# Two of sixteen depthwise-convolution chunks as products with diagonal matrices on TensorE, in a two-layer encoder trunk

## The reference

```python
def conformer_conv(x, w_in, b_in, w_dw, b_dw, ln_g, ln_b, w_out, b_out):
    h = x @ w_in + b_in                       # (1, 256, 4096)
    a, gate = jnp.split(h, 2, axis=-1)
    h = a * jax.nn.sigmoid(gate)
    h = lax.conv_general_dilated(             # depthwise, causal, 31 taps
        h, w_dw, window_strides=(1,), padding=[(CONV_WIDTH - 1, 0)],
        feature_group_count=D_MODEL) + b_dw
    h = layer_norm(h, ln_g, ln_b)             # over the 2048 channels
    h = jax.nn.swish(h)
    return h @ w_out + b_out
```

## Time and profile before

| | |
|---|---|
| median of 3 runs | 3607.17 us (3604.32 to 3616.36) |
| the profiled execution | 3611.92 us, its span 3610.0 us |
| mean granted TensorE clock | 0.908 |
| busy | PE 2933.5 us, DVE 2580.9 us, Pool 1910.6 us, ACT 810.2 us |
| convolution module, up to the first layer norm | about the first 422 us of the span |

### The profile page before, as it was taken

One profiled execution on the slowest core, in us unless ns is written; L12 is line 12 of the kernel. 1 busy time (PEld: TensorE's weight loads), 2 busy tenths in 40 slices (PEclk: granted clock), 3 DMA queues, 4 the chain that ended last, 5 costly groups with the idle time before them and its releaser, 6 DMA issues.

```text
span 3610.0 us, 46542 instructions
## 1 busy us (share of the span) xinstructions
PE 2933.5 (81%) x15209; PEld 2256.1 (62%) x15209; DVE 2580.9 (71%) x3472; ACT 810.2 (22%) x1215; POOL 1910.6 (53%) x1526
## 2 busy tenths in 40 slices
PE   8977895767777789999399998957767777899994
PEld 7864695666767654444198886956666776544441
DVE  4997669787888776666744455697878887766667
ACT  1002431222333420000033443312223334300000
POOL 6795165777777554444300001547777775644443
PEclk9986997888989899999799999978889898999997
DMA  7421446999999669999855435459999997699998
GB/s 248 140 93 41 169 140 253 422 419 422 421 421 422 260 258 410 406 409 409 324 177 186 145 110 183 140 225 423 422 422 421 421 422 283 245 409 406 409 410 319
DMA packets 293734, 1106.84 MB, mean 307 GB/s; under 512 B 21957, under 2 KB 120837, under 8 KB 220677
## 3 DMA queue, kind: packets, MB, share of 16 engines
q0 software_dynamic: 147456, 805.37, 55.1%
q1 hardware_dynamic: 146182, 300.22, 23.1%
HBM read 1103.41 MB, written 2.10 MB: 306 GB/s over the span
## 4 chain that ended last, share of the span: by engine, by line
DMA 41%; PE 24%; DVE 20%; issue 9%; POOL 4%; ACT 1%; DVEq 0%; POOLq 0%; ACTq 0%; SPq 0%
DMA ring<-in_peer_u,index_now 21%; DMA work<-in_peer_v,index_add 14%; PE ps L631 8%; PE ps L651 7%; DMA more_add<-in_peer_v,index_add 6%; DVE work L1218 6%; DVE ps L1467 4%; PE ps L810 3%; POOL ring L544 3%; DVE ring L1424 2%; DVE x_tok L1309 1%; DVE hot_set L1487 1%; PE ps L695 1%; DVE work L1373 1%; DVE work L1370 1%
## 5 line engine op out<-in xcount | busy, mean ns | idle before, releaser
L1424 DVE SCALAR_TENSOR_TENSOR ring<-ring,x_tok 128x2048 f32<-128x2048 f32 x384 | 879.7, 2299 | 229.2 <-DMA ring<-in_peer_u,index_now 221.3
L544 POOL DMA_INDIRECT ring<-in_peer_u,index_now x512 | 843.2, 1647 | 367.1 <-issue 114.9
L849 PE MATMUL ps<-all_v,mix 128*128 128x512 f32 x1984 | 851.8, 592 | 0.0
L849 PEld LDWEIGHTS ps<-all_v,mix 128*128 128x128 f32 x1984 | 377.0, 190 | 474.5 <-issue 474.5
L816 PE MATMUL ps<-x_dot,work 128*128 128x128 f32 x4096 | 536.4, 294 | 94.3 <-ACT work L1066 65.6
L1467 DVE SCALAR_TENSOR_TENSOR ps<-work,coef,ps 128x1024 f32<-128x1024 f32 x344 | 442.2, 1289 | 233.1 <-DMA work<-in_peer_v,index_add 231.3
L810 PE MATMUL ps<-ident,ring 128*128 128x128 f32 x2048 | 348.4, 342 | 311.7 <-DMA ring<-in_peer_u,index_now 306.1
L816 PEld LDWEIGHTS ps<-x_dot,work 128*128 128x128 f32 x4096 | 518.9, 209 | 115.3 <-ACT work L1066 79.8
L810 PEld LDWEIGHTS ps<-ident,ring 128*128 128x128 f32 x2048 | 310.8, 179 | 333.8 <-DMA ring<-in_peer_u,index_now 194.7
L508 POOL TENSOR_TENSOR w_lo<-ring,w_hi 128x2048 fp32r<-128x2048 f32 x34 | 159.2, 4686 | 662.5 <-ACT w_hi L947 662.5
L590 POOL DMA_INDIRECT work<-in_peer_v,index_add x312 | 295.2, 946 | 316.9 <-DVE ps L1467 257.3
(11 more groups left out here) (183 smaller groups left out, 3682.3 us busy)
## 6 DMA issues: line engine op xcount, KB each, us to landing
all_v<-in_peer_v SPq DMA_DIRECT2D x248, 512.0 KB, 6.8
ring<-in_conv_w_in SPq DMA_DIRECT2D x16, 2048.0 KB, 8.8
ring<-in_peer_w_q SPq DMA_DIRECT2D x16, 2048.0 KB, 8.6
ring<-in_attn_w_kv SPq DMA_DIRECT2D x16, 2048.0 KB, 8.6
ring<-in_conv_w_out SPq DMA_DIRECT2D x8, 2048.0 KB, 7.9
ring<-in_attn_w_q SPq DMA_DIRECT2D x8, 2048.0 KB, 8.6
ring<-in_attn_w_o SPq DMA_DIRECT2D x8, 2048.0 KB, 7.9
ring<-in_peer_u,index_now POOLq DMA_INDIRECT x512, 15.0
```

The costliest lines, as they stand in the source:

```text
L544: pool.indirect_dma_start(u_tile(s), None, u_tab, bass.IndirectOffsetOnAxis(ap=index_now[:, half, s:s + 1], axis=0)).then_inc(u_row[s], 16)
L849: mm = pe.matmul(ps[:, dense_bank(tb, q), :], mix[tb][:, row, :], tile[:, q * 512 - HALF:(q + 1) * 512 - HALF], start=False, stop=True, sk ...
L1424: dve.scalar_tensor_tensor(out=u_tile(s), in0=u_tile(s), scalar=1.0, in1=x_tok[:, tb, :], op0=ALU.mult, op1=ALU.mult, accum_out=coef[:, tb ...
```

## The change

- Chunks 14 and 15 are convolved by PE: for each of 31 taps one product of a 128x128 diagonal matrix, which holds that tap of the 128 channels, with a shifted window of 256 columns of the gated, padded chunk, all accumulated in one PSUM bank (bank 4 or 5). ACT builds the diagonal matrices with 31 scaled copies of the identity for each chunk (`diagonals`): those of chunk 14 ahead of its sigmoids, those of chunk 15 after the last sigmoid. DVE takes each result from PSUM with one instruction that adds the bias and subtracts `pilot`.
- Chunk 12 goes from Pool to DVE. Pool has chunks 0, 4 and 8, DVE has eleven, PE two.
- The gates of the last group are moved: DVE gates 11, 12, 13 and 14 one behind the other ahead of the taps of chunk 11, and chunk 15 after them. Then follow chunk 12, the two results of PE, and chunk 13.
- PE convolves chunk 14 directly behind `hidden`, then chunk 15, then adds up twelve chunks (`EARLY_SUMS`), and only then writes the six residual banks; the sums of 12, 14, 15 and 13 follow.
- `load_rows(0)` moves on SP's queue from behind the first four panels to behind the second panel of `conv_w_out`, with a wait for PE's first chunk, because the matrices of chunk 14 lie in `ln_rows`. Those of chunk 15 lie in ring slot 2, so ACT's first rounding waits for PE's second chunk.

```diff
-CONV_ORDER = (0, 1, 2, 3, 4, 5, 6, 7, 9, 10, 11, 8, 13, 14, 12, 15)
+CONV_ORDER = (0, 1, 2, 3, 4, 5, 6, 7, 9, 10, 11, 8, 12, 14, 15, 13)
+SHIFT_ORDER = (9, 10, 11, 12, 14, 15, 13)
+PE_CHUNKS = (14, 15)
+EARLY_SUMS = 12
...
+        tap_diag = [nc.alloc_sbuf_tensor_at("tap_diag0", [P, W, P], F32, offset=ln_rows_at),
+                    nc.alloc_sbuf_tensor_at("tap_diag1", [P, W, P], F32, offset=ring_at + 4 * 2 * 2 * D)]
...
+        more_pad = view(18432, 3, PAD + S)
...
-            load_rows(0)
             sp.dma_start(bias_row[0:1, :], conv_b_out).then_inc(bias_loaded, 16)
...
                 load_split(conv_w_out[0], P_OUT + p, p, True)
+                if p == 1:
+                    sp.wait_ge(pe_conv, 1)
+                    load_rows(0)
...
-            convolve(2, 4)
+            convolve(2, 3)
...
             hidden(2, 4)
 
+            for n, k in enumerate(PE_CHUNKS):
+                pe.wait_ge(diag_ready, n + 1)
+                pe.wait_ge(glu_done, 4 + k + 1)
+                for w in range(W):
+                    mm = pe.matmul(ps[:, Q + n, 0:S], tap_diag[n][:, w, :], more_pad[:, 1 + n, w:w + S], start=(w == 0), stop=(w == W - 1))
+                mm.then_inc(pe_conv, 1)
...
-            pe.wait_ge(glu_done, 4 + KC)
-            pe.wait_ge(bias_loaded, 16)
-            for b in range(6):
-                residual_bias(b // Q, b % Q)
             pe.wait_ge(ch_steps, 1)
             for n, k in enumerate(CONV_ORDER):
+                if n == EARLY_SUMS:
+                    pe.wait_ge(glu_done, 4 + KC)
+                    pe.wait_ge(bias_loaded, 16)
+                    for b in range(6):
+                        if b >= Q:
+                            wait_shifted(pe, PE_CHUNKS[b - Q])
+                        residual_bias(b // Q, b % Q)
...
+            def diagonals(n):
+                for w in range(W):
+                    at = w * KC + PE_CHUNKS[n]
+                    last = act.activation(tap_diag[n][:, w, :], ident[:, :], ACT.Copy, scale=taps[:, at:at + 1])
+                last.then_inc(diag_ready, 1)
+            act.wait_ge(consts, 9)
+            diagonals(0)
...
+            act.wait_ge(proj, IN_HALVES)
+            diagonals(1)
...
                 if k == CONV_ORDER[-1]:
+                    act.wait_ge(pe_conv, 2)
                     for u in range(2):
                         round_half(U_OUT + u)
...
+            def convolve_last():
+                feed_pool(2)
+                for b in range(1, 4):
+                    at = (2 * 3 + b) * STEPS
+                    dve.wait_ge(conv_steps, at)
+                    gated(2, b, hpad[:, b % 2, PAD:])
+                    if b == 3:
+                        gated(3, 0, hpad[:, 0, PAD:])
+                        gated(3, 1, more_pad[:, 0, PAD:])
+                        gated(3, 2, more_pad[:, 1, PAD:])
+                    chunk_steps(2, b, at, hpad[:, b % 2, :], b % 2, True)
+                gated(3, 3, more_pad[:, 2, PAD:])
+                dve.wait_ge(conv_steps, 10 * STEPS)
+                chunk_steps(3, 0, 10 * STEPS, hpad[:, 0, :], 0, True)
+                for n, k in enumerate(PE_CHUNKS):
+                    dve.wait_ge(pe_conv, n + 1)
+                    dve.scalar_tensor_tensor(out=conv[:, k, :], in0=ps[:, Q + n, 0:S], scalar=vec[:, NB_IN + k:NB_IN + k + 1], in1=pilot,
+                                             op0=ALU.add, op1=ALU.subtract).then_inc(shifted, 1)
+                dve.wait_ge(conv_steps, 11 * STEPS)
+                chunk_steps(3, 1, 11 * STEPS, more_pad[:, 0, :], 1, True)
```

More of the change, by code:

```diff
@@ L236, in build @@
         conv_steps = sem("conv_steps")
+        diag_ready, pe_conv = sem("diag_ready"), sem("pe_conv")
         ch_stat, ch_steps, ch_act = sem("ch_stat"), sem("ch_steps"), sem("ch_act")
@@ L335, in wait_shifted @@
                 eng.wait_ge(shifted, k + 1)
-            elif k % 4 == 0:
-                eng.wait_ge(pool_free, 1 + k // 4 + 1)
+            elif k == KC // 2:
+                eng.wait_ge(pool_free, KC // 8 + 2)
             else:
-                eng.wait_ge(shifted, KC // 2 + (3 * (k // 4 - 2) + k % 4))
+                eng.wait_ge(shifted, KC // 2 + SHIFT_ORDER.index(k) + 1)
         block = ctx.enter_context(nc.Block())
@@ L1184, in _ @@
             dve.sem_inc(glu_done, 4)
+            dve.memset(more_pad[:, :, 0:PAD], 0.0)
             dve.memset(hpad[:, :, 0:PAD], 0.0).then_inc(conv_steps, W + 1)
@@ L1190, in _, with column, gated, feed_pool @@
             STEPS = W + 1
+            def column(at):
+                return vec[:, bass.ds(at, 1)] if not isinstance(at, int) else vec[:, at:at + 1]
+            def gated(i, b, to):
+                dve.wait_ge(sig_ready, i * 4 + (b + 1))
+                dve.scalar_tensor_tensor(out=to, in0=ps[:, b, 0:S], scalar=column(i * 4 + b),
+                                         in1=sig[:, b % 2, :], op0=ALU.add, op1=ALU.mult).then_inc(glu_done, 1)
+            def feed_pool(i):
+                dve.wait_ge(pool_free, i + 1)
+                gated(i, 0, pool_pad[:, PAD:])
+                dve.tensor_copy(pool_tap[:, 0:W], taps_by[:, :, bass.ds(i * 4, 1)].rearrange("p w c -> p (w c)")) \
+                   .then_inc(pool_fed, 1)
+                dve.tensor_copy(pool_tap[:, W:], column(i * 4 + NB_IN)).then_inc(pool_fed, 1)
@@ new lines, in chunk_steps @@
+            def chunk_steps(i, b, at, pad, e, shift):
+                dve.tensor_copy(tap_c[:, e, :], taps_by[:, :, bass.ds(i * 4 + b, 1)].rearrange("p w c -> p (w c)")) \
+                   .then_inc(conv_steps, 1)
+                dve.wait_ge(conv_steps, at + 1)
+                dve.wait_ge(glu_done, i * 4 + (4 + b + 1))
+                dve.tensor_scalar(acc_c[:, e, :], pad[:, 0:S], tap_c[:, e, 0:1],
+                                  column(i * 4 + (NB_IN + b)), ALU.mult, ALU.add).then_inc(conv_steps, 1)
+                chunk = conv[:, bass.ds(i * 4 + b, 1), :].rearrange("p a b -> p (a b)")
+                for w in range(1, W):
+                    dve.wait_ge(conv_steps, at + (1 + w))
+                    dve.scalar_tensor_tensor(out=acc_c[:, e, :] if w < W - 1 else chunk, in0=pad[:, w:w + S], scalar=tap_c[:, e, w:w + 1],
+                                             in1=acc_c[:, e, :], op0=ALU.mult, op1=ALU.add).then_inc(conv_steps, 1)
+                if shift:
+                    dve.wait_ge(conv_steps, at + STEPS)
+                    dve.tensor_tensor(out=chunk, in0=chunk, in1=pilot, op=ALU.subtract).then_inc(shifted, 1)
@@ L1191, in convolve @@
             def convolve(first, last):
                 with dve.Fori(first, last) as i:
[L1193 to L1200, removed]
@@ L1201, in convolve @@
-                    dve.tensor_copy(pool_tap[:, 0:W], taps_by[:, :, bass.ds(i * 4, 1)].rearrange("p w c -> p (w c)")) \
-                       .then_inc(pool_fed, 1)
-                    dve.tensor_copy(pool_tap[:, W:], vec[:, bass.ds(i * 4 + NB_IN, 1)]).then_inc(pool_fed, 1)
-                    for b in range(1, 4):
[L1205 to L1223, removed]
@@ new lines, in convolve @@
+                    feed_pool(i)
+                    for b in range(1, 4):
+                        at = i * (3 * STEPS) + b * STEPS
+                        dve.wait_ge(conv_steps, at)
+                        gated(i, b, hpad[:, b % 2, PAD:])
+                        chunk_steps(i, b, at, hpad[:, b % 2, :], b % 2, False)
+            def convolve_last():
+                feed_pool(2)
+                for b in range(1, 4):
+                    at = (2 * 3 + b) * STEPS
+                    dve.wait_ge(conv_steps, at)
+                    gated(2, b, hpad[:, b % 2, PAD:])
[13 more added lines that the diff above has]
+                chunk_steps(3, 1, 11 * STEPS, more_pad[:, 0, :], 1, True)
@@ L1233, in _ @@
                 dve.tensor_tensor(out=c, in0=c, in1=pilot.unsqueeze(1).to_broadcast([P, 4, S]), op=ALU.subtract).then_inc(shifted, 4)
-            convolve(2, 4)
+            convolve_last()
             dve.wait_ge(ch_stat, 2)
@@ L1253, in divide @@
                 dve.tensor_tensor(out=c, in0=c, in1=ch_rstd[:, 0:1, :].to_broadcast([P, 4, S]), op=ALU.mult).then_inc(ch_steps, 1)
-            dve.wait_ge(shifted, KC - 2)
+            dve.wait_ge(shifted, KC - 1)
             dve.wait_ge(squared, KC)
```

## The result

The changed kernel takes 3584.28 us (median of 4 runs, 3577.08 to 3588.42), beside it the kernel before 3611.24 us: a ratio of 0.9925, with a 95% interval of 0.9909 to 0.9940. It is 27 us faster, between 22 and 33. A second set of runs gave 0.9930 (0.9916 to 0.9943). The profiled execution took 3584.70 us, its span 3583.0 us, mean clock 0.920 (before 0.908).

What follows compares the result with a forecast made beforehand. DVE's chain to the last gate, then PE's queue, bound the kernel. DVE's mean 33.4 us earlier took profiled 3611.9 to 3578.5 us; less 4.7 for the median of runs, 3574 us, range 3566 to 3589, chance 0.60.

Steps and rivals of the forecast that it cites:

- The bound and the way of the gain: Convolution: DVE's chain sets the last gate, PE's queue behind it the end; PE's idle 46 us gets filled.
- Diagonal products at 0.216 us a record: PE's chunks 14 and 15 behind `hidden`: 62 records each at full clock, 13.4 us a chunk, ending at 270.5 us.
- Two rivals, in which zeros cost the clock: Clock falls in the diagonal products: regained in the sums, 3599 to 3608 us, or not, 3622; chance 0.03 each.
- The one-hot row: Later stage's one-hot products, nearly all zeros, ran at clock 1.00; taken as reason to expect full-speed diagonal products.
- ACT's copies: Building diagonal matrices: 0.30 us a copy, 9.3 us for 31, neither set making PE late.
- DVE: DVE from 223.60 us: taps of chunks 11, 12 and 13, the last slowed 8.2 us by Pool; shifted at 296.2.
- Nothing given back later: Later stages start by waits, so all 33.4 us pass through; the rival, 3590 to 3607 us, had chance 0.06.
- at full clock one costs 2.11 us, so 12.6 us to 293.5: PE's six residual banks behind the early sums, 12.6 us at full clock in place of 24.0 before.
- The first rival: Clock falls at 286.8 us in the residuals; DVE's mean at 305.8, gain 23 us, 3584 us; chance 0.28.
- they began cold, these begin warm: Argument that the residuals, at half clock for 24 us before, would now keep the full clock.
- the milestone: Start of DVE's copy of the mean, forecast at 296.8 us in place of 330.22, 33.4 us earlier.
- PE and DVE come out even, so a slip of either is felt in full: End of the convolution: PE's last sums at 296.1 us and DVE's last chunk at 296.2 finish together.

Runs made afterwards that it cites:

- 1: Kernel before, with only PE's order changed: twelve early sums ahead of the six residual banks; 3602.67 us, ratio 0.9979.
- 4: Changed kernel, the six residual banks doing the diagonal product twice and leaving out the bias; 3581.66 us, one run.
- 9: The changed kernel measured again without any edit, in a later set; 3583.98 us, ratio 0.9930 to the kernel before.
- 7: Changed kernel, chunk 14 gated behind chunk 11's taps and chunk 13 convolved before PE's second result is taken; 3582.77 us, ratio 0.9919.
- 3: Changed kernel, bias products over 128 rows, 127 of the bias tile's rows zero, in place of one row; 3572.88 us, ratio 0.9896.
- 6: Kernel before, with only the bias products widened from one row to 128 rows, 127 of them zero; 3601.08 us, ratio 0.9968.
- 2: Changed kernel without early sums: six residual banks directly behind PE's two chunks, then all sixteen sums; 3583.41 us, ratio 0.9919.
- 12: Changed kernel with 128-row bias products and the residual banks spread over the early sums; 3573.92 us, ratio 0.9896.
- 5: Changed kernel, one-row bias products kept, one residual bank behind every two of the twelve early sums; 3574.48 us, ratio 0.9900.

## Why the prediction came out as it did

Where the steps held:

- *The bound and the way of the gain.* DVE's chain and PE's queue behind the last gate: shown by 1 (order alone, 10 us at the mean) and by the new chain, which is PE alone from 200 to 303 us.
- *Diagonal products at 0.216 us a record.* 124 records in 26.8 us, clock 1.00: the term was 26.8. Two rivals, in which zeros cost the clock, fall with this row and with 4. The one-hot row, from another stage, had been the right one to go by.
- *ACT's copies* 9.15 us for 31 (forecast 9.3), covered both times.
- *DVE.* Chunk 11 took 17.54 us of taps (forecast 8.4 + 9.1), chunk 12 15.59 (15.7), chunk 13 with Pool's remainders 23.86 (15.7 + 8.2); ready at 297.1 us (296.2).
- *Nothing given back later.* 3179.8 us from layer norm to the end, 3178.6 before.

The step that failed is "at full clock one costs 2.11 us, so 12.6 us to 293.5", with the sums behind it, which the forecast also had at the full clock. The six banks took 15.9 us (3.3 more), and from their end to the mean went 4.8 us in place of 3.3, partly at the half clock: at the mean that is 4.8 us in all. How much of it falls in the banks differs by execution: in 9 and in 7 they took 12.6 and 12.5 us, as forecast, and only the sums behind them were slow (4.9 and 5.0 us). The first rival, the clock falling in the residuals, is what happened in the profiled execution, and its time, 3584, is the measured one; I had given it 0.28 and the forecast 0.60. The weights were wrong, because the row against it, 24.0 us of a busy PE at 0.50, was set aside with "they began cold, these begin warm". The stretch holds the same products in both kernels, and with full rows it kept the clock from warm (3) and gained it from cold (6). The Trainium skill ("TensorE: Matmul & The Clock Gate", Part 1) has the clock follow how busy the engine has been; in 281.9 to 290.6 us the profile has PE busy without a gap, and the clock fell. Busy time as this trace shows it is not the measure: 3 and 4 keep the same busy time and the clock.

The rival's size was off too, and its 3584 agrees partly by luck. It put the fall at 5.9 us after the last dense work; in the four executions in which six banks with one-row products followed dense work in one stretch it was 6.1 (2), 8.8 (changed), 12.4 (9) and 12.8 us (7), and 5.9 in the short piece before. At the mean it expected 9.0 us and got 4.8 us in the profiled execution. Its gain of 23 us was 4 us too small, and the base turned out 4 us higher, which makes the two times equal. A further 1.0 us is the whole chain's later begin (PE's diagonal products at 244.7, not 243.7), which varied by 1.9 us among the executions. 33.4 - 4.8 - 1.0 = 27.6, which is what the milestone shows. The median is lower by 27.0 us, 6.4 less than the forecast's gain. The other 4 us between 3574 and 3584 are the base: the three runs of before known then had a median of 3607.2, with the fourth 3611.2.

What the forecast called even, "PE and DVE come out even, so a slip of either is felt in full", is confirmed from both sides: PE's slip by the clock was felt (5.53 us of waiting on DVE), and without it DVE's last chunk sets the mean: PE waits 2.23 us for it in 3 and 12 and is just ready in 5. Then 53.2 us pass from PE's start, in place of 57.9 or, in 9, 54.6 us: 4.7 or 1.4 us come back, no more.

## What to carry to other kernels

When work moves to an engine that then has no idle time left, ask next what that engine's longest remaining stretch does to its own clock, not only what it costs at the clock it has now; the stretch that had stayed at the half clock before, though the engine was busy, lost the clock here although it began warm. Spread one-row products among dense ones, or fill their rows with zeros: here both held the clock, and neither made the kernel slower. And an edit's worth depends on what is idle: the early sums gave 10 us where PE waited, and next to nothing where it did not.

## What the runs showed of the hardware

- One-row products that alternate pair by pair with full ones over 512 columns did not hold the clock. A PE busy with them stayed at 1.2 GHz for 24.0 us, and went from 2.4 to 1.2 GHz in 6.1 to 12.8 us. With a diagonal matrix, or with 127 rows of zeros, in place of the one row the same stretch held it: clock 1.00 for 10.3 us (3, 4), and up from cold in 3.3 us (6). Whether the one row or the alternation does it was not taken apart.
- A one-row product between full ones is slower than a full one: 1.05 us a pair of records against 0.86 us, for the full product beside it as well. The weight loads of the changed kernel and of 3 differ there (PE's weight loads, start us, us, idle before):

```profile
283.87 0.30 PEld L677 LDWEIGHTS ps<-x_tok,alpha_ident 128*128 128x128 f32 x2 [0.76 <-issue]
284.93 0.29 PEld L727 LDWEIGHTS ps<-work,ones 1*128 1x128 f32 x2 [0.76 <-issue]
```

```profile
283.18 0.19 PEld L729 LDWEIGHTS ps<-work,ones 128*128 128x128 f32 x1 [0.24 <-issue]
283.61 0.19 PEld L679 LDWEIGHTS ps<-x_tok,alpha_ident 128*128 128x128 f32 x1 [0.24 <-issue]
```

  In the first the loads come two together after 0.76 us, in the second evenly. Why the alternation costs 0.19 us was not tried.
- Beside each of Pool's two subtractions of 128x2048 (9.34 us together) one DVE instruction with two inputs took 4.6 us in place of about 0.5: two taps in the changed kernel, one tap and L1223 in the kernel before. Thirty taps took 23.86 us with two of them and 15.59 us without.
